# Fourth mixer of a two-layer hybrid block: copies ahead of the chain of states in halves, a state step with fewer instructions in it, the bonus steps in the second inversion, gate and head-sum products between the steps of the chain

## The reference, cut to what matters

```
def step(S, xt):
    r_t, w_t, k_t, v_t, a_t, b_t = xt
    sa = einsum('bhvk,bhk->bhv', S, a_t)
    S = S * w_t[:, :, None, :] + sa[..., None] * b_t[:, :, None, :] + v_t[..., None] * k_t[:, :, None, :]
    return S, einsum('bhvk,bhk->bhv', S, r_t)
```

```
y = _norm(y, gn_g, gn_b, eps=RWKV_LNX_EPS)
bonus = sum(rh * (dirs[0][2] + dirs[1][2]) * rk, axis=-1, keepdims=True) * vh
out = (y + bonus).reshape(g.shape) * g          # g = sigmoid(gd) @ g2
```

## Time and profile before

| | value |
|---|---|
| median of three runs | 1881.91 us |
| profiled execution: span from first to last instruction | 1869.7 us (the page lists no time around it) |
| PE busy | 1656.7 us, 89% |
| DVE, ACT, POOL busy | 58%, 34%, 4% |
[...]
| layer 0: chain of d=0 and of d=1, with what follows up to the next inversion or y | 565 to 589, 635 to 658 us |
| layer 1: the same | 1535 to 1555, 1600 to 1617 us |
| DVE: bonus steps | 1.23; two of 0.44; 1.22; two of 0.75 us |
| DVE: one copy of 512 columns from PSUM; ACT the same | 0.68; 0.59 us |
| POOL: six masks between the directions | 2.28 us |
| DMA of one block of w_out, issue to landing | 3.7 us |

### The profile page before, as it was taken

One profiled execution on the slowest core, in us unless ns is written; L12 is line 12 of the kernel. 1 busy time (PEld: TensorE's weight loads), 2 busy tenths in 40 slices (PEclk: granted clock), 3 DMA queues, 4 the chain that ended last, 5 costly groups with the idle time before them and its releaser, 6 DMA issues. The chain is left out here.

```text
span 1869.7 us, 29418 instructions
## 1 busy us (share of the span) xinstructions
PE 1656.7 (89%) x12114; PEld 1302.6 (70%) x12114; DVE 1093.6 (58%) x1870; ACT 632.9 (34%) x1052; POOL 82.8 (4%) x112
## 2 busy tenths in 40 slices
PE   6999999688778899999999979999967778879996
PEld 4667776565577678888877757778753677668875
DVE  2384456985755575554443365735686755578765
ACT  4344322433121136222232253433334211166651
POOL 0000011200201000000000000000201100000000
PEclk8999999898697799999999989998978788789999
DMA  9311211373201033222222022112152001155550
GB/s 389 115 57 35 68 57 45 120 256 123 93 2 47 24 135 125 101 95 104 95 90 90 1 93 80 57 57 91 46 187 77 34 2 48 46 195 204 188 198 28
DMA packets 41620, 182.01 MB, mean 97 GB/s; under 512 B 4752, under 2 KB 5520, under 8 KB 33680
## 3 DMA queue, kind: packets, MB, share of 16 engines
q1 hardware_dynamic: 41488, 180.14, 27.1%
HBM read 179.08 MB, written 1.05 MB: 96 GB/s over the span
## 5 line engine op out<-in xcount | busy, mean ns | idle before, releaser
L235 PE MATMUL ps<-hr_in,wr_in 128*128 128x512 f32 (+1 forms) x544 | 223.0, 410 | 14.6 <-DVE wr_in L228 13.4
L236 PE MATMUL ps<-hr_in,wr_in 128*128 128x512 f32 (+1 forms) x544 | 210.7, 387 | 0.0
L237 PE MATMUL ps<-hr_in,wr_in 128*128 128x512 f32 (+1 forms) x544 | 210.5, 387 | 0.0
L235 PEld LDWEIGHTS ps<-hr_in,wr_in 128*128 128x128 f32 x544 | 109.9, 202 | 64.5 <-issue 36.2
L228 DVE TENSOR_TENSOR wr_in<-mix,wr_in 128x1024 fp32r<-128x1024 f32 x68 | 83.9, 1235 | 95.3 <-ACT wr_in L224 92.4
L235 PE MATMUL ps<-mix_r,work_r 128*128 128x512 f32 (+1 forms) x352 | 136.3, 387 | 1.6 <-DVE work_r L228 1.6
L236 PE MATMUL ps<-work_r 128*128 128x512 f32 (+1 forms) x356 | 135.7, 381 | 0.0
L228 DVE TENSOR_TENSOR work_r<-pr,work_r 128x2048 fp32r<-128x2048 f32 x38 | 87.0, 2289 | 72.1 <-ACT work_r L224 68.0
L237 PE MATMUL ps<-mix_r,work_r 128*128 128x512 f32 x320 | 127.2, 398 | 0.0
L2843 PE MATMUL ps<-mix_r,work_r 128*128 128x512 f32 x336 | 121.4, 402 | 2.3 <-DVE mix_r L228 2.3
L237 PEld LDWEIGHTS ps<-hr_in,wr_in 128*128 128x128 f32 x544 | 109.5, 201 | 19.8
(11 more groups left out here) (505 smaller groups left out, 3392.2 us busy)
## 6 DMA issues: line engine op xcount, KB each, us to landing
mix<-in_w_in SPq DMA_DIRECT2D x68, 512.0 KB, 3.6
pr<-in_w_up SPq DMA_DIRECT2D x28, 1024.0 KB, 4.9
pr<-in_ada_w SPq DMA_DIRECT2D x44, 512.0 KB, 6.2
ring<-in_w_up SPq DMA_DIRECT2D x16, 1024.0 KB, 4.8
ring<-in_ada_w SPq DMA_DIRECT2D x28, 512.0 KB, 4.5
pr<-in_w_down SPq DMA_DIRECT2D x14, 1024.0 KB, 4.9
pr<-in_ada_w SPq DMA_DIRECT2D x8, 1024.0 KB, 15.6
work<-in_w_out SPq DMA_DIRECT2D x16, 512.0 KB, 3.7
```

The lines of the kernel that those rows point to most:

```text
L235: nc.tensor.matmul(out, sh, mh, start=first, stop=False)
L236: nc.tensor.matmul(out, sh, ml, start=False, stop=False)
L237: return nc.tensor.matmul(out, sl, mh, start=False, stop=last)
```

## The change

- PE, AkT·v and Q: semaphores per half. P has its own semaphore for ACT. DVE copies the first half of Qp and of Q, ACT the second. In d=0 the raw blocks 0 and 1 stand between AkT·v and Q, their DVE copies between the two half copies; raw block 3 stands in the second step and raw block 2 after the first state product.
- The chain starts when the first half of Q is copied; the second half is waited for by DVE at the second step.
- The state product is split: kT·vT is issued before the wait for U, beT·U after it. DVE multiplies the old state by the decay ahead of the wait, and then does product times decay plus that in one instruction per half.
- In d=1 the gate halves' matmuls stand one after a state product and one before it, the head sums before the last u-product's successor; their order is in the diff. The bonus steps go to units 1, 3, 4 and 6 of the second inversion and write `al` in place of `ks` and `rr`. Low parts 0 and 1 of the weights stand behind the first and second state, 2 and 3 behind the sum of y; ACT's high parts 0 and 1 stand between its copies to Qp and Q.
- In d=0 the solve products of d=1 stand ahead of both halves of y; the diagonals stand in the third and fourth step. POOL masks the blocks of d=1 first and writes the level masks after.
- `keep_busy` is 2 in both layers. The wait for all raw copies stands behind the x0 products.

```diff
-    RAW_STEP = ((0, 1), (2,), (3,), ())
-    LOW_AT = ((), (0,), (1,), (2, 3))
-    BONUS_AT = ((0, 1), (2,), (3,), ())
+    LOW_AT = ((0,), (1,), (), ())
+    BONUS_AT = (1, 3, 4, 6)
+    BONUS_BANK = (3, 2)
...
@@ PE @@
-            pe.wait_ge(S("raw_out"), len(RAW0))
...
+                if d == 0:
+                    pe.wait_ge(S("raw_out"), len(RAW0))
...
-                if d and layer == 0:
-                    keep_busy(5, ps[0][:, :])
+                if d:
+                    keep_busy(2, ps[0][:, :])
...
+                mm.then_inc(S("p"), 1)
                 for j in range(TILES):
                     for hd in range(HEADS):
                         mm = nc.tensor.matmul(ps[j // 2][...], mat(AkT, j, hd), vT[...], start=True, stop=True)
-                mm.then_inc(S("pq"), 1)
-                pe.wait_ge(S("qp_out"), d + 1)
+                    if j % 2:
+                        mm.then_inc(S("pq"), 1)
+                if d == 0:
+                    raw_next(0)
+                    raw_next(1)
                 for j in range(TILES):
+                    if j % 2 == 0:
+                        pe.wait_ge(S(("qp_a", "qp_b")[j // 2]), d + 1)
                     for hd in range(HEADS):
                         mm = nc.tensor.matmul(ps[2 + j // 2][...], mat(XT, j, hd), Qp[...], start=True, stop=True)
-                mm.then_inc(S("q"), 1)
-                pe.wait_ge(S("q_out"), d + 1)
+                    if j % 2:
+                        mm.then_inc(S("q"), 1)
+                pe.wait_ge(S("q_a"), d + 1)
...
-                    for k in RAW_STEP[m] if d == 0 else ():
-                        raw_next(k)
+                    if m < TILES - 1:
+                        into_state(j, kT, vT, True)
+                    if d == 0 and m == 1:
+                        raw_next(3)
                     if d and m in (1, 2):
...
+                        gate(m - 1, True)
+                    if d and m == 3:
+                        bonus_sum(1)
                     if m:
                         pe.wait_ge(S("u"), (TILES - 1) * d + m)
                     if m < TILES - 1:
...
-                        mm.then_inc(S("s_mm"), 1)
+                        into_state(j, beT, U if m else Q, False).then_inc(S("s_mm"), 1)
+                    if d == 0 and m == 0:
+                        raw_next(2)
+                    if d and m < 2:
+                        gate(m, False)
+                    if d and m == 2:
+                        pe.wait_ge(S("q_b"), 2)
+                        bonus_sum(0)
                 if d == 0:
+                    solve(1)
                     pe.wait_ge(S("raw1_out"), 3)
-                else:
-                    pe.wait_ge(S("bonus"), 1)
-                    head_sums(E, pe, rr, (2, 3), layer).then_inc(S("bonus_mm"), 1)
                 for i in range(2):
-                    if d == 0 and i == 1:
-                        solve(1)
@@ DVE @@
+                    if d == 1 and u in BONUS_AT:
+                        bonus(BONUS_AT.index(u))
                 dve.wait_ge(S("x_up"), (NU + TILES) * (d + 1))
-                dve.wait_ge(S("pq"), d + 1)
-                nc.vector.tensor_copy(Qp[:, 0:512], ps[0][:, :])
-                nc.vector.tensor_copy(Qp[:, 512:1024], ps[1][:, :]).then_inc(S("qp_out"), 1)
-                dve.wait_ge(S("q"), d + 1)
+                dve.wait_ge(S("pq"), 2 * d + 1)
+                nc.vector.tensor_copy(Qp[:, 0:512], ps[0][:, :]).then_inc(S("qp_a"), 1)
+                if d == 0:
+                    raw1_out(0)
+                    raw1_out(1)
+                dve.wait_ge(S("q"), 2 * d + 1)
                 dve.wait_ge(S("pt_out"), d + 1)
...
+                nc.vector.tensor_copy(Q[:, 0:512], ps[2][:, :]).then_inc(S("q_a"), 1)
...
                         if m:
-                            link(nc.vector.tensor_tensor(new, old, ps[2][:, 0:P], ALU.add))
+                            for i in range(2):
+                                ins = nc.vector.tensor_scalar(kept_state[:, half_of[i]], old[:, half_of[i]], decay[i], None, ALU.mult)
+                            link(ins)
+                        if d == 0 and m == 2:
+                            diagonal(1, (0, 1))
+                        dve.wait_ge(S("s_mm"), (TILES - 1) * d + m + 1)
                         for i in range(2):
...
+                            if m:
+                                ins = nc.vector.scalar_tensor_tensor(out=new[:, half_of[i]], in0=ps[2][:, half_of[i]], scalar=decay[i],
+                                                                     in1=kept_state[:, half_of[i]], op0=ALU.mult, op1=ALU.add)
+                            else:
+                                ins = nc.vector.tensor_scalar(new[:, half_of[i]], ps[2][:, half_of[i]], decay[i], None, ALU.mult)
                         ins.then_inc(S("s"), 1)
-                    for k in RAW_STEP[m] if d == 0 else ():
-                        raw1_out(k)
-                if d == 0:
-                    diagonal(1)
+                    if d == 0 and m < 2:
+                        raw1_out(2 + m)
+                    if d == 0 and m >= 2:
+                        diagonal(1, (m,))
+                    for n in LOW_AT[m] if d else ():
+                        weight_low(n)
...
@@ ACT @@
-                act.wait_ge(S("pq"), d + 1)
+                act.wait_ge(S("p"), d + 1)
...
+                act.wait_ge(S("pq"), 2 * d + 2)
+                nc.scalar.copy(Qp[:, 512:1024], ps[1][:, :]).then_inc(S("qp_b"), 1)
+                if d:
+                    act.wait_ge(S("x_up"), 2 * (NU + TILES))
+                    weight_high(0)
+                    weight_high(1)
+                act.wait_ge(S("q"), 2 * d + 2)
+                nc.scalar.copy(Q[:, 512:1024], ps[3][:, :]).then_inc(S("q_b"), 1)
+            weight_high(2)
+            weight_high(3)
```

More of the change, by code:

```diff
@@ L2155, in _, with gate, bonus_sum, into_state @@
                                               Qp[:, j * 256 + hd * HD:j * 256 + (hd + 1) * HD], start=True, stop=True)
-                mm.then_inc(S("q"), 1)
-                pe.wait_ge(S("q_out"), d + 1)
+                    if j % 2:
+                        mm.then_inc(S("q"), 1)
+                def gate(i, rest):
+                    if rest:
+                        nc.tensor.matmul(ps[6 + i][:, lo0:], par[0:32, Q_LORA + 768 + i * P:Q_LORA + 768 + (i + 1) * P],
+                                         pr[0:32, T_GD2 * T + lo0:(T_GD2 + 1) * T], start=False, stop=True).then_inc(S("gate"), 1)
+                    else:
+                        nc.tensor.matmul(ps[6 + i][:, lo0:], par[:, Q_LORA + 512 + i * P:Q_LORA + 512 + (i + 1) * P],
+                                         pr[:, T_GD * T + lo0:(T_GD + 1) * T], start=True, stop=False)
+                def bonus_sum(i):
+                    pe.wait_ge(S("bonus"), 1)
+                    head_sum(E, al, i, BONUS_BANK[i], layer).then_inc(S("bonus_mm"), 1)
+                def into_state(j, lh, rh, first_):
+                    for i in range(2):
+                        for q in range(2):
+                            a = j * 256 + (2 * i + q) * HD
+                            mm = nc.tensor.matmul(ps[2][q * HD:(q + 1) * HD, i * HD:(i + 1) * HD], lh[:, a:a + HD], rh[:, a:a + HD],
+                                                  start=first_ and i == 0, stop=not first_ and i == 1)
+                    return mm
+                pe.wait_ge(S("q_a"), d + 1)
                 for m, j in enumerate(ORDER[d]):
@@ L2349, in _, with weight_low @@
                 coefficients(nc, E, modb, JOBS[q], ps[7][:, 8 * q:8 * q + 8]).then_inc(S("sums_out"), 1)
+            def weight_low(n):
+                dve.wait_ge(O("w_high"), n + 1)
+                parts.low(nc, dve, n, SIDE, T)
+                split_low(nc, dve, parts.raw(n), parts.weight(n, 0), parts.weight(n, 1)).then_inc(O("w_low"), 1)
             def raw0_out(k):
@@ L2353, in raw0_out, with diagonal @@
                 raw_out(0, *RAW0[k], bank0(k)).then_inc(S("raw_out"), 1)
-            def diagonal(d):
-                for j in range(TILES):
+            def diagonal(d, js_):
+                for j in js_:
                     dve.wait_ge(S("own"), TILES * d + j + 1)
@@ L2385, in _ @@
                 raw0_out(k)
-            diagonal(0)
+            diagonal(0, range(TILES))
             raw0_out(TILES)
@@ L2443, in _ @@
                         ins.then_inc(S("u"), 1)
-                    for step in BONUS_AT[m] if d else ():
-                        bonus(step)
-                    for n in LOW_AT[m] if d else ():
-                        dve.wait_ge(O("w_high"), n + 1)
-                        parts.low(nc, dve, n, SIDE, T)
-                        split_low(nc, dve, parts.raw(n), parts.weight(n, 0), parts.weight(n, 1)).then_inc(O("w_low"), 1)
                     if m < TILES - 1:
-                        dve.wait_ge(S("s_mm"), (TILES - 1) * d + m + 1)
```

73 lines of the change are left out of this document (35 added, 38 removed).

## The result

The changed kernel takes 1825.19 us, median of five runs (1823.66 to 1832.30), against 1880.65 for five of the kernel before: ratio 0.9717, interval 0.9694 to 0.9739. The two profiled executions differ by less: spans of 1825.7 and 1869.7, 44.0 apart, with a mean granted clock of 0.931 and 0.915 of full speed.

The account below looks back on a forecast made before the run. One strand of PE and DVE steps handing over to each other was taken to bound the kernel. Savings 1.5 + 1.3 + 1.2 + 9.0 + 7.4 + 5.4 + 12.0 − 2 = 35.8 off 1881.9 gave 1846 us, range 1828 to 1866.

Parts of the forecast that it names:

- rival 2: The clock holds through the d=1 chain, with no holes from P to y: about 50 us saved, 1832 us; chance 0.15.
- Copies by halves: P to chain, both layers: closed holes and part of the clock's gain save 9.0 us in d=0, 7.4 in d=1.
- The chain in d=1: First state product to y: PE fed without a hole, 6.5 + 5.5 = 12.0 us saved, near the low end.
- The chain in d=0 and its solve: From the chain to the next inversion: 3.7 us saved in layer 0, 1.7 in layer 1, sum 5.4.
- the walks at the two levels: d=0 chain to next inversion, from T, the first state product's end: T+17.6 and T+16.4 full level, T+22 and T+19 low.
- The masks: POOL masks after the blocks: 2.3 us of POOL, needed about 10 us later, so cost 0; even 6 us fits.
- Fillers ahead of P: keep_busy 5 to 2 in layer 0 saves 1.3 us; 0 to 2 in layer 1 saves 1.2, bounds 0 to 1.5.
- x0 ahead of the wait: First inversion, layer 0: two tiles' records done under the raw copies, 1.5 us saved, bounds 0 to 1.8; layer 1 0.
- Bonus in the inversion: Bonus steps in the second inversion: 4.7 us of DVE per layer hidden by its idle time, cost 0; without cover 4.7.
- Weight parts behind y: Weight parts 2 and 3, 1.6 us each on DVE ahead of the mean steps: charged 1 per layer, bound 0 to 3.
- time lost outside the stretches: Sign that the forecast as a whole is wrong: time lost outside the four stretches from P through the chains.
- the base: Savings were taken off 1881.91 us, the median of three runs, 12.2 above the profiled execution's span of 1869.7.

Follow-up runs that it names:

- the copies-alone kernel: The kernel before with only the copies to Qp and Q by halves, shared by DVE and ACT: 1852.19 us, ratio 0.9863.
- separate gates: The changed kernel with both gate parts together between the u and state products and the head sums behind the chain: 1839.24 us, ratio 0.9779.

## Why the prediction came out too small

The mechanism was the right one and its size was off: rival 2, which I gave 0.15, is what happened. The step that failed is the price of the clock level: I counted half of its gain ahead of the chain and a quarter of it in the chain of d=1 (12.0 between 9.3 and 20.3), and the runs gave all of it ahead of the chain and nearly all in it. By the prediction's own terms, from the two traces:

- *Copies by halves.* d=0 9.0 forecast, 13.4 measured (6.54 + 6.83); d=1, with the 1.2 for the fillers of layer 1, 8.6 forecast, 11.2 measured (4.48 + 6.75). I took half of the clock's part; all of it came, in every one of the four stretches, and the two sums lie 0.6 and 0.5 above my high ends, 12.8 and 10.7.
- *The chain in d=1*: 12.0 forecast, 19.6 measured (11.98 + 7.57), upper end 20.3. This is the term that failed most, and the sentence behind it was "The clock stayed low here though PE was busy 6.16 of 7 us, so I stay near the low end". The run with the Qp hole put back shows that this row proves nothing about the level without holes: with PE busy 22.00 of 22 the level stayed low too when it was low at entry, and the same work kept the full level when it had it. I read as a property of the work what was a state handed on from the holes in front.
- *The chain in d=0 and its solve*: 5.4 forecast, 3.15 measured (2.66 + 0.49). I took a value between the walks at the two levels. DVE is the limit here, PE has holes, and the level fell at about 567.7; x0 came at T+21.0 and T+18.9, beside the T+22 and T+19 of the walk at the low level. I had left out the two kept-state instructions' stretching beside POOL (0.66 + 0.78). Moving them to ACT gave back 4.4 us of medians. The masks cost nothing: they ran from 567.97 to 570.26 beside reductions of DVE that took their usual 0.64 each, and were over before DVE's solve began. For the kept state the trace shows only that each pair ends just behind POOL's block; that the block is the cause isn't shown, since no run takes it away.
- *Fillers ahead of P*: 1.3 in layer 0 forecast, 1.0 measured in the inversion's stretch. In layer 1 they removed the 2.05 of idle and P takes 1.97 instead of 3.45. I priced the two at 2.5; leaving both out costs 13.5 in medians, with a wide spread (5 to 31 over the four runs), and 19.2 in the stretches of the one trace.
- *x0 ahead of the wait*: 1.5 forecast, nothing left at the end: from the solve to P 47.20 before, 47.23 after. It did gain 0.9: DVE's MEMSET near the end of the inversion starts 36.50 after the solve instead of 37.44. That was lost again behind it: over 538 to 542 the granted clock is 0.50, where it was 0.61 before. I had no term for the level there.
- *Bonus in the inversion*: 0, and 0 measured for the inversions. What it frees in the chain, 8.7 us once the level is held, I had inside the chain's term as about 1.0 of wait per layer.
- *Weight parts behind y*: −2 forecast; from y of d=1 to the last split of a weight in layer 0 34.7 before and 34.4 after, so no loss.
- *What the level is worth in a product.* 32 records of AkT·v of layer 1 take 3.79 at a granted 1.00 and 7.09 at 0.50, in the two traces of the kernel before.

The stretches and the inversions add up to 47.9 less, against 44.0 between the spans, since 3.9 were lost outside them. The prediction named time lost outside the stretches as a sign against it; these 3.9 are within what that code varies by from trace to trace. The other part of the miss is the base: I took the savings of a quick execution of before off a median that holds slower ones. Two more traces, one of before and one with only the bonus moved, show the stretches 7.4 and 5.0 longer; that this is all of it isn't shown.

## What to carry to other kernels

Look for the short hole ahead of a long run of PE work, not at the busy share inside it: two waits of 1.45 us cost 9 to 27 us here, 18 by the medians, and two filler products or a copy split between two engines are enough to close one. Price an edit with its neighbours: the bonus steps were worth nothing while other holes kept the level low and 8.7 us when they were the last ones. Where a trace shows a stretch at the low level, price it at both levels, and put the chance by what stands in front of it.

## What was unexpected of the hardware

- The granted clock has a memory in this work: with equal instructions PE stayed at 0.50 for 22 us at a busy share of 100%, or at 1.00 for the whole chain.
- Its return isn't settled by the work alone. In two traces of the kernel before, the same products followed the same hole of 2.05 in layer 1. The level was back after some 3 us in one; in the other it stayed at 0.50 through 10.7 us of P and AkT·v without a gap. Without the fillers it was some 3 us behind 1561.68 and about 40 behind 603.81. Why is open.
- The length of a hole doesn't decide alone. From the full level, those of 1.29, 1.38, 1.45, 1.94, 2.05 and 3.04 that were looked at were followed by a fall, in the hole or within 2 us of it. Of the short ones 1.08 ahead of P in the changed kernel was not; 1.05 and 0.67 one after the other in its d=0, 1.07 in the copies-alone kernel, and holes of 0.65 and 0.66 with separate gates were. Two holes of 0.32 in d=1 of layer 1 were followed by a fall in the kernel after and not in the two with fillers in d=0.
- Two DVE instructions of 64 columns from SBUF to SBUF went from 0.41 to 1.07 and 1.19 beside one POOL instruction of 1.10, ending 0.20 and 0.32 behind it.
